# Pairs of heads in a two-layer block's attentions, and ten modulation chunks moved from them into the second projection

## The chip, the cores and the metric

The kernel runs on one core of one Trainium2 chip. The metric is the device time of one execution in microseconds (us). Names of engines: PE is TensorE, DVE VectorE, ACT ScalarE, POOL GpSimd, SP SyncE, which issues most of the transfers.

## The reference, cut to what matters

Two transformer blocks of two layers each work on 256 latent tokens and 256 context tokens of width 1024, in float32. The change touches the first block only. Each of its layers computes, in this order, six modulation vectors, a projection, four mixers side by side (a Fourier mix, "diff" attention, neighbourhood attention "na", a gated MLP along chunks), an output projection and a convolutional feed-forward network. The two attentions are what is changed:

```
m_lat = split(silu(c)     @ w_ada[li] + b_ada[li], 6)      # modulation: 6 x 1024 numbers per stream
m_ctx = split(silu(c_ctx) @ w_ada[li] + b_ada[li], 6)
p, pc = h @ w_in[li], hc @ w_in[li]                          # latent and context tokens
# diff attention, 4 heads: two softmaxes over 32 dimensions each
s = einsum('bhcqd,bhckd->bhcqk', q, k) * 32**-0.5;  a = softmax(s)
o = einsum('bhqk,bhkd->bhqd', a[:, :, 0] - lam * a[:, :, 1], v)      # v has 64 columns per head
# na attention, 4 heads of 64: latent queries see a window (as a bias) and all of the context
a = softmax(concat([q k_local + bias, q k_ctx]) * ...);  o = a v
# context queries (first layer only) see the 256 context keys
```

## The kernel before

**Stream.** All big weights lie in one list of chunks of 1 MB (1024 x 256 floats). SP loads them in order into a ring of four slots (L1155); a slot is free when PE has multiplied with it. A modulation weight is a chunk like any other ("ada" chunk). There are 96 of them for both blocks, and a table of parts (ADA_PARTS) says where in the stream, and so where in PE's program, each is multiplied: 8 at the start, 16 in the first layer's projection, 22 in the first layer's attentions, 17 in the second layer's attentions, the rest in gaps and later. `pe_ada` (L267) does one chunk by eight matmuls of 256 columns whose stationary operands are 32 columns wide, spread over four groups of 32 output partitions of bank 7. The chunks are gathered in batches; when a batch is full ACT copies it to SBUF (L311) and PE turns it by a small matmul (L291) into bank 7's second half.

**Projection.** `pe_in1` multiplies nine chunks of 256 columns with h (L233, L358), and behind some of them does a small piece of the mixers (`pe_slot`: Fourier L383, L392, L393, gMLP L404, square sums L423 and L432). In the first layer two ada chunks follow each of the first eight; in the second none. ACT copies the results out (L732).

**Attentions.** A unit is one head and 128 queries. There are 16 units for the latent queries (eight diff, eight na; 512 keys) and, in the first layer only, 16 more for the context queries (256 keys). All three engines go through the units in a pipeline whose order is written out:

- PE, step u: scores of unit u+1 (L493; for diff two matmuls with 32 rows each, for na one with 64 rows; two sets of two banks in turn), an ada chunk in some steps (L267), transposes of unit u-1 (L505, four or two of 128x128), values of unit u-2 (L520). The values' stationary operand is 128 columns wide and covers two heads; the output is 128 partitions, of which 64 are used.
- DVE: for unit u the add of the window bias (na with latent queries, L595) and the negated maximum (L598); for unit u-1 the reciprocal of the row sums (L609) and the weights (diff L613, L614, L616; na L619); for unit u-3 the copy of the 64 used output partitions to y (L628).
- ACT: for unit u the exponentials with their row sums (L556), for unit u-1 the copy of the transposed weights to WT (L568).

Semaphores tie them: scores of unit u+2 wait for the exponentials of unit u, transposes for the weights, values for the copy to WT and for the copy of the values before. Behind the last unit DVE squares the diff outputs (L838), PE sums them (L670) and goes on to the output projection (L663).

## Time and profile before

| | us |
|---|---|
| median of three runs | 2966.58 (2956.06 to 2972.48) |
| the profiled execution | 2964.01 |
| its span, first to last instruction | 2962.2 |
| mean granted PE clock | 0.979 of full |

| engine | busy us | share |
|---|---|---|
| PE matmul | 2822.7 | 95% |
| PE weight load (beside it) | 2232.1 | 75% |
| DVE | 1575.8 | 53% |
| POOL | 926.6 | 31% |
| ACT | 675.4 | 23% |

The span is from the first to the last instruction of one profiled execution; 1.8 us lie around it. Busy shares are means over stages of different kinds. The chain that ended last is followed back from the last instruction; in each stage it says which engine set the end. A line of it has a start, a length and how many records are merged ("x4"). A float32 matmul leaves two records, a transpose one. The granted clock is the share of full clock that PE was given; 1.00 is 2.4 GHz, 0.50 is 1.2 GHz.

### The profile page before, as it was taken

Reading aid. Unit: us, or ns where it says so; the run is one execution under the profiler, and the core shown is the slowest. Engines: PE = TensorE matmul, PEld = TensorE weight load, DVE = VectorE, ACT = ScalarE, POOL = GpSimd, SP = SyncE. Lnnn points to the kernel's source line nnn. Section 1 sums busy time; section 2 is a strip of 40 time slices with the busy share of each in tenths; the row PEclk is TensorE's granted clock in tenths of the full one; section 3 lists DMA queues with packets and bytes.
Section 4 is the critical chain, followed back from the end, with each engine's and each line's share of the span. In section 5 each row is a group of like instructions: output and inputs, shape, how many; then the busy total and the mean of one; then the engine's idle time right before and its main releaser. Section 6 shows DMA issues by size and latency. Waiting matters only on the chain.

```text
span 2962.2 us, 41023 instructions
## 1 busy us (share of the span) xinstructions
PE 2822.7 (95%) x16033; PEld 2232.1 (75%) x16033; DVE 1575.8 (53%) x2664; ACT 675.4 (23%) x1386; POOL 926.6 (31%) x705
## 2 busy tenths in 40 slices
PE   7999999999899999999978889999999999999999
PEld 3566488888666799744448889788688886698899
DVE  2237378773235588555567775684545122224772
ACT  1124121110123221133235555320100002321000
POOL 1000045554200166300134442553455440020565
PEclk8999999999999999999999999999999999999999
DMA  7447222222415544534432231312122223111443
GB/s 292 170 170 259 111 73 92 92 86 100 156 71 211 188 157 170 207 141 164 124 97 76 73 87 40 118 72 86 71 90 95 86 86 130 60 44 44 152 163 127
DMA packets 108360, 357.82 MB, mean 121 GB/s; under 512 B 41200, under 2 KB 60400, under 8 KB 69136
## 3 DMA queue, kind: packets, MB, share of 16 engines
q1 hardware_dynamic: 86432, 334.65, 32.1%
q10 hardware_dynamic: 20160, 15.40, 1.6%
q0 software_dynamic: 1584, 5.21, 0.6%
q8 instruction: 127, 2.08, 0.3%
q14 instruction: 57, 0.47, 0.1%
HBM read 344.62 MB, written 10.62 MB: 120 GB/s over the span
## 4 chain that ended last, share of the span: by engine, by line
PE 81%; DVE 9%; ACT 4%; DVEq 2%; issue 2%; DMA 2%; POOLq 0%; POOL 0%; ACTq 0%; SPq 0%
PE psum L2955 38%; PE psum L233 16%; PE psum L358 4%; PE psum L267 3%; PE psum L663 3%; PE psum L2506 2%; PE psum L493 1%; ACT h_sb L1116 1%; PE psum L520 1%; DMA ring<-in_stream 1%; PE psum L1640 1%; PE psum L1622 1%; PE psum L2607 1%; PE psum L505 1%; DVE arena L1063 1%
## 5 line engine op out<-in xcount | busy, mean ns | idle before, releaser
L2955 PE MATMUL psum<-arena,ring 128*128 128x256 f32 (+1 forms) x3128 | 559.1, 331 | 0.9 <-DVE arena L3033 0.9
L2955 PEld LDWEIGHTS psum<-arena,ring 128*128 128x128 f32 x3128 | 488.8, 191 | 45.0 <-DVE arena L3033 1.5
L233 PE MATMUL psum<-h_sb,ring 128*128 128x512 f32 (+1 forms) x1248 | 480.3, 543 | 20.7 <-ACT h_sb L1116 18.0
L233 PEld LDWEIGHTS psum<-h_sb,ring 128*128 128x128 f32 x1248 | 238.9, 194 | 250.6 <-issue 228.1
L2955 PE MATMUL psum<-arena,c 128*128 128x256 f32 (+1 forms) x1952 | 359.2, 333 | 1.7 <-DVE c L2974 1.7
L2955 PEld LDWEIGHTS psum<-arena,c 128*128 128x128 f32 x1952 | 308.8, 191 | 31.6 <-issue 1.9
L2983 POOL TENSOR_TENSOR rows<-ring 128x512 f32<-128x512 f32 (+1 forms) x70 | 89.8, 1283 | 621.6 <-DVE arena L3013 333.5
L2983 POOL TENSOR_TENSOR c<-ring 128x512 f32<-128x512 f32 (+1 forms) x73 | 95.1, 1303 | 597.6 <-PE psum L2955 283.9
L2955 PE MATMUL psum<-h_sb,ring 128*128 128x256 f32 (+1 forms) x1264 | 227.5, 334 | 1.0 <-DVE arena L1063 0.8
L2985 POOL TENSOR_TENSOR ring<-ring 128x512 f32<-128x512 f32 x143 | 216.1, 1511 | 23.4 <-issue 3.5
L2999 ACT COPY kst<-psum 128x256 f32<-128x256 f32 (+1 forms) x99 | 31.7, 320 | 837.1 <-PE psum L2955 812.2
L2955 PEld LDWEIGHTS psum<-h_sb,ring 128*128 128x128 f32 x1264 | 199.6, 193 | 20.5 <-issue 1.9
L2987 POOL TENSOR_TENSOR c<-ring 128x512 f32<-128x512 f32 x143 | 205.8, 1439 | 20.3
L2140 DVE SCALAR_TENSOR_TENSOR arena<-psum,vec,arena 128x508 f32<-128x508 f32 (+1 forms) x128 | 95.6, 747 | 106.3 <-ACT arena L1849 98.7
L358 PE MATMUL psum<-ring,h_sb 128*128 128x256 f32 x512 | 118.7, 393 | 9.2 <-ACT h_sb L1116 9.2
L267 PE MATMUL psum<-ring,silu_w 128*32 128x256 f32 x1536 | 106.4, 405 | 18.7 <-DMA ring<-in_stream 11.8
L3045 DVE TENSOR_TENSOR h_sb<-kst,psum 128x256 f32<-128x256 f32 (+1 forms) x20 | 7.3, 365 | 215.0 <-ACT kst L2999 215.0
L358 PEld LDWEIGHTS psum<-ring,h_sb 128*128 128x128 f32 x512 | 98.2, 195 | 31.1 <-ACT h_sb L1116 7.2
L267 PEld LDWEIGHTS psum<-ring,silu_w 128*32 128x32 f32 x1536 | 43.0, 113 | 88.1 <-issue 45.0
L2955 PE MATMUL psum<-arena,rows 128*128 128x256 f32 (+1 forms) x552 | 105.3, 333 | 0.3 <-POOL gates L2990 0.3
L2955 PEld LDWEIGHTS psum<-arena,rows 128*128 128x128 f32 x552 | 88.3, 191 | 8.6 <-POOL gates L2990 0.7
L2091 POOL TENSOR_TENSOR arena<-arena,c 128x512 f32<-128x512 f32 x12 | 17.0, 1440 | 239.7 <-DMA arena<-gsums 239.7
(362 smaller groups left out, 4418.1 us busy)
## 6 DMA issues: line engine op xcount, KB each, us to landing
ring<-in_stream SPq DMA_DIRECT2D x302, 1024.0 KB, 4.8
arena<-decays SPq DMA_DIRECT2D x24, 256.0 KB, 4.9
ring<-gsums SPq DMA_DIRECT2D x20, 256.0 KB, 4.2
keys_d<-kst ACTq DMA_DIRECT2D x16, 256.0 KB, 3.9
arena<-gsums SPq DMA_DIRECT2D x12, 256.0 KB, 4.3
x_sb<-in_x ACTq DMA_DIRECT2D x1, 2048.0 KB, 19.2
arena<-in_rpb POOLq DMA_DIRECT2D x32, 64.0 KB, 8.4
keys_d<-c ACTq DMA_DIRECT2D x8, 256.0 KB, 5.0
```

The lines of the kernel that those rows point to most:

```text
L233: ins = pe.matmul(out_ap, lhs(k), rhs(k), start=first and k == 0, stop=last and k == nk - 1)
L267: ins = pe.matmul(bank(7)[32 * j:32 * (j + 1), 0:256], silu[:, a // (2 * ADA_CHUNKS), k, ADA_ROWS - 2 - 2 * q:2 * ADA_ROWS - 2 - 2 * q], w ...
L358: ins = pe.matmul(bank(rho % 4)[:, tt * 256:(tt + 1) * 256], h[:, k, tok:tok + 128], w[:, slot, k, :], start=k == 0, stop=k == KT - 1)
L493: ins = pe.matmul(bank(2 * (u % 2) + c)[:, 0:TOK - st * SEQ], queries[p:p + width], keys[p:p + width], start=True, stop=True)
L663: ins = pe.matmul(bank(rho % 4)[:, 0:tok], w[:, n % RING, k, rho % 2 * 128:(rho % 2 + 1) * 128], y[:, k, 0:tok], start=first and k == ks[0 ...
L2140: ins = dve.scalar_tensor_tensor(z[:, :, lo:hi], u[:, :, lo + shift:hi + shift], b["v"]("dn_conv", 1, 20 * j + 5 * q + 2 + shift), z[:, :, ...
L2506: ins = pe.matmul(bank(rho % 2)[:, tt * 256:(tt + 1) * 256], h[:, k, tok:tok + 128], w[:, (n0 + c) % RING, k, :], start=k == 0, stop=k == ...
L2955: ins = pe.matmul(dst, self.seven_weights(n, i, k, nk), self.seven_moving(x, sums, i, k, nk, width), start=first and j == 0 and k == 0, st ...
L2983: pool.tensor_tensor(s3, a11, a21, ALU.subtract)
L2985: pool.tensor_tensor(a21, a21, a22, ALU.add)
L2987: ins = pool.tensor_tensor(s2, a21, a11, ALU.subtract)
L2999: act.copy(self.out1[:, 0:width], self.seven_bank(item, 0)[:, 0:width]).then_inc(T["first_copied"], 1)
```

## The change

1. Units of na hold two heads: their scores are two matmuls with 64 rows each, on the upper and lower half of the array's rows, in two banks; one maximum, one reciprocal, two scalings and two runs of transposes serve the pair. Units of diff stay one head, but their order is now: both heads of a pair for the same 128 queries, one behind the other.
2. Values are done for two heads at a time: for each 128 keys two matmuls with stationary operands of 64 columns, to output partitions 0-63 and 64-127 of bank 6. All 128 partitions are used; one copy to y for two heads. `WT` becomes two areas with room for two heads each.
3. The first layer has 24 units instead of 32, the second 12 instead of 16. The ada chunks (22 in the first layer) are spread evenly over them.
4. Of the second layer's 17 ada chunks ten are multiplied in its projection instead (two behind each of the first two chunks, one behind each of the next six), seven stay in the attentions. Two batches are turned ahead of the first of the seven. The last square sum of the projection waits for the copy of the batch (ada_copied 6), since it overwrites bank 7.

```diff
 QKV_ADA = [3] * 4 + [2] * 4
-ADA_PARTS = _spans([("ada_first", MIX_ADA), ("ada_in1", 16), ("ada_next0", 22), ("gap1", 2), ("gap2", 4),
-                    ("ada_next1", 17), ("gap3", 3), ("gap4", 4), ("ada_last", sum(QKV_ADA))])
+ADA_PARTS = _spans([("ada_first", MIX_ADA), ("ada_in0", 16), ("ada_next0", 22), ("gap1", 2), ("gap2", 4),
+                    ("ada_in1", 10), ("ada_next1", 7), ("gap3", 3), ("gap4", 4), ("ada_last", sum(QKV_ADA))])
 GAP_AHEAD = {"gap1": 2, "gap2": 0, "gap3": 1, "gap4": 2}
 ADA_BATCHES = [(0, 8), (8, 24), (24, 36), (36, 48), (48, 52), (52, 62), (62, 72), (72, 84), (84, 96)]
+IN1_ADA = ((2, 2, 2, 2, 2, 2, 2, 2, 0), (2, 2, 1, 1, 1, 1, 1, 1, 0))
 TURNED_AT_END = ("ada_first", "gap1", "gap3", "ada_last")
 ADA_ROWS = 2 * max(_end - _first for _first, _end in ADA_BATCHES)
 SILU_COLS = 2 * ADA_ROWS - 2
...
-        WT = area(19456, 1024, z2=2, k=4)
+        WT = [area(at, 1024, z2=2, k=4) for at in (19456, 26560)]
...
@@ -258,7 +261,9 @@
 
             n, a = ada_at(name, i)
             batch, q, last = ada_batch(a)
-            if a > 0 and q == 0 and a not in [ADA_PARTS[part][1] for part in TURNED_AT_END]:
+            if a == ADA_PARTS["ada_in1"][1]:
+                pe_turn(pe, batch - 2)
+            if a > 0 and q == 0 and a not in [ADA_PARTS[part][1] for part in TURNED_AT_END + ("gap2",)]:
                 pe_turn(pe, batch - 1)
             arrived(pe, n)
             for half in range(2):
...
@@ -362,9 +367,8 @@
                         tok = in1_tokens(li, c)
                         k_products(pe, bank(rho % 4)[:, 0:tok], lambda k: w[:, slot, k, half * 128:(half + 1) * 128],
                                    lambda k: h[:, k, 0:tok])
-                if li == 0 and c < IN1_CHUNKS - 1:
-                    for i in range(2):
-                        pe_ada(pe, "ada_in1", 2 * c + i)
+                for i in range(IN1_ADA[li][c]):
+                    pe_ada(pe, f"ada_in{li}", sum(IN1_ADA[li][:c]) + i)
                 pe_slot(pe, li, c)
 
         def pe_slot(pe, li, c):
@@ -425,7 +429,7 @@
                 ins.then_inc(S["rot_ready"], 1)
                 pe.wait_ge(S["qk_sq"], 3 * li + 3)
                 pe_qk_sum(pe, 6, 6)
-                pe.wait_ge(S["ada_copied"], 2 if li == 0 else 5)
+                pe.wait_ge(S["ada_copied"], 2 if li == 0 else 6)
                 pe_qk_sum(pe, 7, 7).then_inc(S["qk_sum"], 1)
 
         def pe_qk_sum(pe, n, b):
@@ -480,46 +484,50 @@
                     dve_square(dve, rho, streams)
 
         def pe_attention(pe, li, units, u0):
+            t0 = 2 * G0[li]
+
             def scores(u):
-                kind, st, hd, qt = units[u]
-                g = u0 + u
+                kind, st, heads, qt = units[u]
                 if u >= 2:
-                    pe.wait_ge(S["exp_done"], g - 1)
-                keys = P[:, (4 if kind == "diff" else 10) + hd // 2, st * SEQ:TOK]
-                queries = P[:, (2 if kind == "diff" else 8) + hd // 2, st * SEQ + qt * 128:st * SEQ + qt * 128 + 128]
-                width, count = (32, 2) if kind == "diff" else (64, 1)
-                for c in range(count):
-                    p = (hd % 2) * 64 + c * 32
+                    pe.wait_ge(S["exp_done"], u0 + u - 1)
+                keys = P[:, (4 if kind == "diff" else 10) + heads[0] // 2, st * SEQ:TOK]
+                queries = P[:, (2 if kind == "diff" else 8) + heads[0] // 2, st * SEQ + qt * 128:st * SEQ + qt * 128 + 128]
+                width = 32 if kind == "diff" else 64
+                for c in range(2):
+                    p = (heads[0] % 2) * 64 + c * width
                     ins = pe.matmul(bank(2 * (u % 2) + c)[:, 0:TOK - st * SEQ], queries[p:p + width], keys[p:p + width],
                                     start=True, stop=True)
                 ins.then_inc(S["scores_ready"], 1)
 
             def transposes(u):
-                kind, st, hd, qt = units[u]
-                g = u0 + u
-                pe.wait_ge(S["weights_ready"], g + 1)
-                if u >= 2:
-                    pe.wait_ge(S["wt_ready"], g - 1)
+                kind, st, heads, qt = units[u]
                 nk = 4 - 2 * st
-                for k in range(nk):
-                    ins = pe.transpose(bank(4 + u % 2)[:, k * 128:(k + 1) * 128],
-                                       EXPO[:, u % 2, 0, k * 128:(k + 1) * 128], ident[:, :])
-                ins.then_inc(S["wt_psum"], 1)
+                for c, hd in enumerate(heads):
+                    t = head_of(units, u) + c
+                    pe.wait_ge(S["weights_ready"], t0 + t + 1)
+                    if t >= 2:
+                        pe.wait_ge(S["wt_ready"], t0 + t - 1)
+                    for k in range(nk):
+                        ins = pe.transpose(bank(4 + hd % 2)[:, k * 128:(k + 1) * 128],
+                                           EXPO[:, u % 2, c, k * 128:(k + 1) * 128], ident[:, :])
+                    ins.then_inc(S["wt_psum"], 1)
 
             def values(u):
-                kind, st, hd, qt = units[u]
-                g = u0 + u
-                pe.wait_ge(S["wt_ready"], g + 1)
-                if u >= 1:
-                    pe.wait_ge(S["o_copied"], g)
+                kind, st, heads, qt = units[u]
+                if heads[-1] % 2 == 0:
+                    return
+                g = head_of(units, u) // 2
+                pe.wait_ge(S["wt_ready"], t0 + 2 * g + 2)
+                if g >= 1:
+                    pe.wait_ge(S["o_copied"], G0[li] + g)
                 nk = 4 - 2 * st
                 vs = 6 if kind == "diff" else 12
-                p = (hd % 2) * 64
                 for k in range(nk):
                     kt = 2 * st + k
-                    ins = pe.matmul(bank(6)[:, 0:128],
-                                    P[:, vs + kt // 2, (kt % 2) * 256 + (hd // 2) * 128:(kt % 2) * 256 + (hd // 2) * 128 + 128],
-                                    WT[:, u % 2, k, :], start=k == 0, stop=k == nk - 1)
+                    for j in range(2):
+                        v0 = (kt % 2) * 256 + (heads[-1] // 2) * 128 + 64 * j
+                        ins = pe.matmul(bank(6)[64 * j:64 * j + 64, 0:128], P[:, vs + kt // 2, v0:v0 + 64],
+                                        WT[g % 2][:, j, k, :], start=k == 0, stop=k == nk - 1)
                 ins.then_inc(S["o_ready"], 1)
...
@@ -584,29 +598,26 @@
             neg_lam = small[:, 4:5]
 
             def maxima(u):
-                kind, st, hd, qt = units[u]
-                g = u0 + u
-                dve.wait_ge(S["scores_ready"], g + 1)
+                kind, st, heads, qt = units[u]
+                dve.wait_ge(S["scores_ready"], u0 + u + 1)
                 b = 2 * (u % 2)
                 n = TOK - st * SEQ
-                count = 2 if kind == "diff" else 1
+                scores = bank(b, 2).rearrange("p (c k) -> p c k", c=2)[:, :, 0:n]
                 if kind == "na" and st == 0:
-                    part = bank(b)[:, 0:SEQ]
-                    dve.tensor_tensor(part, part, NAB[:, hd, qt, :], ALU.add)
+                    part = scores[:, :, 0:SEQ]
+                    dve.tensor_tensor(part, part, NAB[:, heads[0]:heads[0] + 2, qt, :], ALU.add)
                     dve.drain()
-                scores = bank(b, count).rearrange("p (c k) -> p c k", c=count)[:, :, 0:n]
-                dve.tensor_reduce(small[:, 8 + b:8 + b + count], scores, AX.X, ALU.max, negate=True)\
+                dve.tensor_reduce(small[:, 8 + b:10 + b], scores, AX.X, ALU.max, negate=True)\
                    .then_inc(S["max_ready"], 1)
 
             def weights(u):
-                kind, st, hd, qt = units[u]
-                g = u0 + u
-                dve.wait_ge(S["exp_done"], g + 1)
+                kind, st, heads, qt = units[u]
+                dve.wait_ge(S["exp_done"], u0 + u + 1)
                 n = TOK - st * SEQ
                 b = 12 + 2 * (u % 2)
                 r = small[:, 16:18]
                 dve.drain()
-                dve.reciprocal(r[:, 0:2 if kind == "diff" else 1], small[:, b:b + (2 if kind == "diff" else 1)])
+                dve.reciprocal(r, small[:, b:b + 2])
                 dve.drain()
                 e = EXPO[:, u % 2]
                 if kind == "diff":
@@ -616,17 +627,18 @@
                     dve.scalar_tensor_tensor(e[:, 0, 0:n], e[:, 1, 0:n], small[:, 18:19], e[:, 0, 0:n],
                                              ALU.mult, ALU.add).then_inc(S["weights_ready"], 1)
                 else:
-                    dve.tensor_scalar(e[:, 0, 0:n], e[:, 0, 0:n], r[:, 0:1], None, ALU.mult)\
-                       .then_inc(S["weights_ready"], 1)
+                    for c in range(2):
+                        dve.tensor_scalar(e[:, c, 0:n], e[:, c, 0:n], r[:, c:c + 1], None, ALU.mult)\
+                           .then_inc(S["weights_ready"], 1)
 
             def copy_o(u):
-                kind, st, hd, qt = units[u]
-                g = u0 + u
-                dve.wait_ge(S["o_ready"], g + 1)
-                p = (hd % 2) * 64
+                kind, st, heads, qt = units[u]
+                if heads[-1] % 2 == 0:
+                    return
+                dve.wait_ge(S["o_ready"], G0[li] + head_of(units, u) // 2 + 1)
                 tok = st * SEQ + qt * 128
-                dve.tensor_copy(y[p:p + 64, (2 if kind == "diff" else 4) + hd // 2, tok:tok + 128],
-                                bank(6)[p:p + 64, 0:128]).then_inc(S["o_copied"], 1)
+                dve.tensor_copy(y[:, (2 if kind == "diff" else 4) + heads[-1] // 2, tok:tok + 128],
+                                bank(6)[:, 0:128]).then_inc(S["o_copied"], 1)
 
             n = len(units)
             for u in range(n + 3):
@@ -641,11 +653,15 @@
         def units_of(li):
             out = []
             for st in range(2 if li < DEPTH - 1 else 1):
-                out += [(kind, st, hd, qt) for kind in ("diff", "na") for hd in range(4) for qt in range(2)]
+                for half in range(2):
+                    for qt in range(2):
+                        out += [("diff", st, (2 * half + j,), qt) for j in range(2)]
+                out += [("na", st, (2 * half, 2 * half + 1), qt) for half in range(2) for qt in range(2)]
             return out
 
         UNITS = [units_of(li) for li in range(DEPTH)]
         U0 = [0, len(UNITS[0])]
+        G0 = [0, head_of(UNITS[0], len(UNITS[0])) // 2]
 
         def pe_mixers1(pe, li):
...
@@ -3447,10 +3463,9 @@
         w_in = _chunks(i["w_in"][li])[list(IN1_ORDER)]
         if li == 0:
             stream.append(ada[:MIX_ADA])
-            for c in range(IN1_CHUNKS - 1):
-                stream.append(np.stack([w_in[c], *ada[MIX_ADA + 2 * c:MIX_ADA + 2 * c + 2]]))
-            w_in = w_in[IN1_CHUNKS - 1:]
-        stream.append(w_in)
+        for c in range(IN1_CHUNKS):
+            first = ADA_PARTS[f"ada_in{li}"][0] + sum(IN1_ADA[li][:c])
+            stream.append(np.stack([w_in[c], *ada[first:first + IN1_ADA[li][c]]]))
         stream.append(ada[slice(*ADA_PARTS[f"ada_next{li}"])])
         stream.append(_chunks(i["w_out"][li]))
         stream.append(ada[slice(*ADA_PARTS[f"gap{2 * li + 1}"])])
```

## Rows read from the trace of the kernel before

**Rows 1.** Windows: length, busy PE, PEld, DVE, ACT, POOL; clock, DMA share, GB/s.

```profile
914.00:976.00 62.00, 59.24 (x521) 35.04 (x522) 40.98 (x90) 26.21 (x66) 0.00 (x0) 1.00 0.84 305
```

**Rows 2.** The chain: start, us, engine, line, records. Second layer's attentions, 512 keys.

```profile
931.45 1.06 PE psum L493 x4
932.50 1.00 PE psum L267 x16
933.50 0.59 PE psum L505 x4
934.09 0.89 PE psum L520 x8
...
950.17 0.55 PE psum L291 x4
...
956.74 1.05 PE psum L493 x2
```

**Rows 3.** The chain, first layer's attentions of context queries, 256 keys.

```profile
284.96 0.37 PE psum L505 x2
285.33 0.45 PE psum L520 x4
285.78 0.63 PE psum L493 x2
```

**Rows 4.** The chain at the start and end of both attention stretches.

```profile
205.70 1.15 PE psum L493 x4
...
209.64 2.08 PE psum L493 x4
...
212.71 1.87 PE psum L267 x16
...
300.38 3.27 PE psum L670 x4
...
914.18 1.15 PE psum L493 x4
...
975.61 1.98 PE psum L670 x4
```

**Rows 5.** Windows, columns as in rows 1, behind the first scores of both layers.

```profile
212.00:214.00 2.00, 2.00 (x20) 1.17 (x19) 1.76 (x5) 0.00 (x0) 0.00 (x0) 0.50 0.00 0
...
916.00:918.00 2.00, 1.71 (x22) 0.94 (x20) 1.71 (x2) 1.39 (x5) 0.00 (x0) 1.00 0.91 385
```

**Rows 6.** The chain in the first (to 114 us) and second layer's projection.

```profile
72.81 1.86 PE psum L267 x32
...
113.21 0.63 PE psum L392 x2
...
836.76 0.43 PE psum L392 x2
...
853.95 2.50 PE psum L404 x32
...
882.43 13.81 PE psum L358 x64
```

**Rows 7.** VectorE in order of time (start, us, line, operation): three reciprocals.

```profile
921.01 0.17 DVE L609 RECIPROCAL small<-small 128x2 f32<-128x2 f32 x1
...
923.86 0.17 DVE L609 RECIPROCAL small<-small 128x2 f32<-128x2 f32 x1
...
926.90 0.17 DVE L609 RECIPROCAL small<-small 128x2 f32<-128x2 f32 x1
```

**Rows 8.** Groups by line and shape on VectorE, 918 to 975: busy us, mean ns.

```profile
L598 DVE TENSOR_REDUCE small<-psum 128x2 f32<-128x1024 f32 x6 | 7.3, 1219 | 0.8 <-PE psum L493 0.8
...
L598 DVE TENSOR_REDUCE small<-psum 128x1 f32<-128x512 f32 x8 | 5.5, 691 | 0.6
...
L595 DVE TENSOR_TENSOR psum<-psum,arena 128x256 f32<-128x256 f32 x8 | 3.5, 433 | 5.4 <-PE psum L493 5.4
```

**Rows 9.** Rate in 40 slices of 20 to 80 us, early ada chunks and projection.

```profile
GB/s 388 421 399 415 437 421 426 421 399 421 431 429 406 435 408 389 216 194 194 27 0 0 0 0 0 76 377 426 426 426 366 11 0 0 0 27 208 426 421 426
```

More of the change, by code:

```diff
@@ L165, in build_program @@
         DATA1 = CONST1 + C1["end"]
-        assert DATA1 + D1["end"] <= 28672
+        assert DATA1 + D1["end"] <= 26560
         def c1(name, n=128):
@@ L248, in ada_at @@
             first, end = ADA_PARTS[name]
-            if name == "ada_in1":
-                return in1_chunk(0, i // 2) + 1 + i % 2, first + i
+            if name in ("ada_in0", "ada_in1"):
+                li = int(name[-1])
+                c = [i < sum(IN1_ADA[li][:j + 1]) for j in range(IN1_CHUNKS)].index(True)
+                return in1_chunk(li, c) + 1 + i - sum(IN1_ADA[li][:c]), first + i
             if name == "ada_last":
@@ L539, in pe_attention, with head_of @@
                     pe_ada(pe, ada, i)
+        def head_of(units, u):
+            return sum(len(units[i][2]) for i in range(u))
         def next_ada_at(li, u, units):
@@ L561, in copy_wt @@
             def copy_wt(u):
[L562 to L569 removed]
+                kind, st, heads, qt = units[u]
+                nk = 4 - 2 * st
+                for c, hd in enumerate(heads):
+                    t = head_of(units, u) + c
+                    g = t // 2
+                    act.wait_ge(S["wt_psum"], t0 + t + 1)
+                    if g >= 2:
+                        act.wait_ge(S["o_ready"], G0[li] + g - 1)
+                    act.copy(WT[g % 2][:, hd % 2, 0:nk, :], bank(4 + hd % 2)[:, 0:nk * 128].rearrange("p (k q) -> p k q", k=nk))\
+                       .then_inc(S["wt_ready"], 1)
             n = len(units)
```

27 lines of the change are left out of this document (10 added, 17 removed).

## The prediction

> **What bounds the kernel now.** I read the busy shares first, then the chain that ended last over each of the two attention stretches and the projections beside them, then the same seconds on VectorE, then granted clock and DMA by windows. TensorE (PE) is busy over 95% of the span, and in the second layer's attentions 59.2 of 62 us [rows 1]. The chain there is one PE step after the other. A step of a unit with 512 keys is scores 1.06, a modulation chunk 1.00, transposes 0.59, values 0.89 [rows 2]. With 256 keys it is 0.63, 1.00, 0.37, 0.45 [rows 3]. Turning a batch is 0.55. So what PE drops from a step is gained until VectorE or a wait is next. The first layer's attentions run from 205.70 to the sums of squares at 300.38, the second's from 914.18 to 975.61 [rows 4].
>
> **Scores by pairs.** A diff unit has two matmuls on two row groups of 32 (four records) in 1.06; an na unit has one with 64 rows (two records) in 1.05 [rows 2]. The two halves of diff thus run at once, and I price a pair of na heads, on rows 0-63 and 64-127 and in two banks, like diff: 1.06 for two heads (0.63 with 256 keys). Eight na pairs with 512 keys save 8 x 1.05 = 8.4, four with 256 keys 4 x 0.63 = 2.5. By layer: first 4.2 + 2.5, second 4.2.
>
> **Values by pairs.** Today each head multiplies both heads' columns and half is thrown away: two heads cost 1.78 (0.90). New: eight matmuls with 64 columns each, alternating between two column halves of one bank. No row shows just that, so bounds. Below: perfect overlap, half of 1.78, is 0.89. Above: no overlap, 1.78 + 0.2 for the change of tile shape = 1.98. Between lie two rows. The modulation chunk alternates four column groups: 16 records of 256 columns in 1.00. At the plain rate, 13.81 for 64 such records [rows 6], they would need 3.45 one after the other, 0.86 four at once: full overlap and 0.14 for the new shape. The gMLP, with 64 columns but four matmuls in a row on one half, needs 2.50 for 16, or 1.25 for eight [rows 6]. Change of shape back costs the next operation 0.2: the same two matmuls take 0.63 behind a chunk and 0.43 without it [rows 6]. The order here alternates as the chunk's does, so I take 0.85 + 0.18 = 1.03 for 512 keys and 0.43 + 0.17 = 0.60 for 256. A saving of 0.75 and 0.30 for each two heads: first layer 8 x 0.75 + 8 x 0.30 = 8.4, second 6.0.
> The Trainium skill speaks against it here: "TensorEngine Tiling (Array Packing)", Key Properties, says that changing the tiling mode drains the engine; the trace agrees, with the 0.2 above. "TensorE: Matmul & The Clock Gate", Measured speedup, has 2.38 times for three column tiles instead of 3; an estimate by that share would be 1.78 / 1.59 = 1.12 for the pair, and 2 us less gain in all.
>
> **First layer.** PE drops 6.7 + 8.4 = 15.1. Its 22 chunks now fall on 24 steps instead of 32. Can the others follow? VectorE's pace is seen where it runs free: reciprocal to reciprocal 2.85, and 3.04 with a copy of an output [rows 7]; the copy is now in every second unit, so 2.95. PE's mean diff step is 1.06 + 1.00 + 0.59 + 0.52 = 3.17: PE still leads. In na pairs VectorE has the add (0.43 for 256, I take 0.70 for 512), one reduction 1.22 for both (two of 0.69 today) [rows 8], small steps and two scalings, together 3.55 by the same spacing; PE has 1.06 + 1.00 + 1.18 + 1.03 = 4.27. With 256 keys PE's diff step is 0.63 + 1.00 + 0.37 + 0.30 = 2.30, and VectorE's 2.95 less at least 0.53 for the shorter reduction, at most 2.4: even. So the first layer gains PE's 15.1. ScalarE has two exponentials and two copies in an na pair, under 3 us, no bound.
>
> **Second layer's attentions.** PE's sum falls by 4.2 + 6.0 + 10 x 1.00 = 20.2. Not all is gained, as VectorE becomes even with PE. Time from the first scores: the third unit's scores start after 3.93 as today; scores, now two turns (1.10), a chunk and transposes end at 7.7; the next scores, reduction and so the third reciprocal are at 10.1; five further reciprocals at 2.95, and 0.7 for the first na add, 25.5; weights and transposes of the last diff unit 27.8. Four na steps of 3.7, 4.2, 3.3 and 2.2 follow (the later of VectorE's 3.55 and PE's 3.27 or, with a chunk, 4.27; the last has neither scores nor chunk), then today's tail of 4.4. Together 45.6 against 61.4: 15.8 less.
> **The clock.** In the first layer PE has nothing from the end of the second scores (two of 1.0 from 205.70) to the third at 209.64, 1.9 us [rows 4]; chunk and turn come behind them. Its granted clock is then 0.50, the 1.2 GHz level [rows 5], and scores take 2.08, the chunk 1.87 [rows 4]. The second layer today has a turn and a chunk in that gap, and its clock stays at 1.00 [rows 5]. With 7 chunks over 12 units its first step has none: the gap becomes the first layer's. From 209.64 to 212.71 + 1.87 and the transposes behind it took 6.0 where full clock has 3.2; with the second turn, that costs 3.1, and VectorE waits for it. I take it: 15.8 - 3.1 = 12.7.
>
> **The projection.** PE takes over ten chunks, and it is the chain there without a gap: nothing hides them. From the first layer: two chunks in a row 1.86, 0.2 behind them [rows 6]. Two places with two, six with one: 2 x 1.86 + 6 x 1.00 + 7 x 0.2 (the gMLP pays none) = 11.1. Their ten loads leave a stretch with 305 GB/s [rows 1]; they queue on SP only behind loads of the same ring, four deep, and a projection chunk with 512 tokens holds PE for 13.8 [rows 6]: time for five loads. The new wait for batch 6's rows before the last square sums has behind it one matmul; ScalarE copies them while PE does the rotation: nothing. If that cover were gone it would be under 1 us.
>
> **Sum.** 15.1 + 12.7 - 11.1 = 16.7. The profiled execution is 2964.0 (span 2962.2, 1.8 around it): 2947.3. It lies 2.6 under the median of the runs; I give **2947**.
>
> **Rivals.** (1) The two column halves do not overlap as taken. At the gMLP's rate a pair costs 1.40 and 0.77: 16 x 0.37 + 8 x 0.17 = 7 us less gain, 2954. Without overlap 19 us less, 2966, no change. For: one 64-column row, below full overlap. Against: the chunk's row. 0.14.
> (2) No fall of the clock in the second layer: 2944. For: a gap of the same length leaves the second layer's clock alone today, if with work behind it; against: the first layer's row shows the very sequence. 0.12.
> (3) **Slower**: the clock stays low through the second layer's attentions. With PE and VectorE even, shorter steps leave PE short idle stretches, and nothing but such steps follows the first gap. PE's 38 us there would be 75, 30 more than the 46 counted: 2964 + 12 = 2976. It decides from where lost stretches like the first layer's (2.8 us each) number six beyond the one counted. Against: today's narrow steps with 256 keys keep the clock. 0.05.
> (4) Transfers: the first layer's last eleven chunks come every 2.4 us. The chip delivers up to 437 GB/s [rows 9], a chunk in 2.4 us: just even, with four in the ring. At today's 305 GB/s it is 3.4 us, 11 x 1.0 less the ring's lead of some 3: 8 us, 2955. 0.08.
> (5) The change doing nothing of what it says, heads paired but run one after the other on row groups: 11 us less, 2958. 0.02.
> Forecast: 0.57; 0.02 for what I don't see.
>
> **Numbers.** About 0.5%, 15 us, is what a measurement of this kernel can tell from none; the threshold is 2951.7, only 5 under my value, and the three runs shown spread over 16. Forecast band 2939 to 2955, three quarters of it faster. 0.57 x 0.75 + 0.12 x 0.9 + shares of (1) and (4) 0.07 + (5) 0.01 = 0.62 faster, 0.34 same, 0.04 slower. Range: down to 2937 (no fall of the clock, full overlap at 0.89, a fast run), up to 2961 (gMLP rate or transfers, a slow run).
>
> **What would show it.** In the changed profile's chain: scores of an na pair 1.06 with four records; values of a pair at 1.03 (1.4 for rival 1); the first layer's attentions some 79 us from first scores to sums of squares, the second's some 48.7 (45.6 without the clock's fall); the second projection 11 us longer; clock 0.5 behind the second layer's second scores, 1.00 after some 6 us; waits of PE for a landing in the first layer for rival 4. I am wrong if values aren't near 1.03, if VectorE's waits grow in the first layer too, or if the clock falls elsewhere.

## The result and the profile after

The changed kernel takes 2945.15 us (median of 8 runs, 2941.53 to 2951.49) beside 2967.23 of the kernel before on the same chips (8 runs, 2956.06 to 2972.72): a ratio of 0.9931, 95% interval 0.9912 to 0.9950. It is faster, by 22 us in the medians; the profiled executions differ by 18.8 (spans 2962.2 and 2943.4). 2947 had been forecast, with a range of 2937 to 2961.

Where the span's 18.8 us went, by the chains of both kernels (an attention stretch is from its first scores to the first matmul of the squares' sum; the projection from its first matmul to the start of the last copy of its results):

| stretch | before | after | difference | forecast |
|---|---|---|---|---|
| first layer's attentions | 94.68 | 77.16 | -17.5 | -15.1 |
| second layer's projection | 122.33 | 133.45 | +11.1 | +11.1 |
| second layer's attentions | 61.43 | 50.36 | -11.1 | -12.7 |
| the rest of the span | | | -1.3 | 0 |

The rest is 0.5 us less ahead of the first attentions, 1.7 more between them and the second projection, and 2.5 less behind the second attentions.

The chain of the changed kernel in the first layer's attentions is still one PE step behind another. Its lines (start, us, engine, line, records) of a step in the na part, first with 512 keys, then with 256:

```profile
240.72 1.06 PE psum L498 x4
241.78 1.00 PE psum L272 x16
242.78 1.02 PE psum L511 x8
243.80 1.02 PE psum L529 x16
...
270.54 0.63 PE psum L498 x4
271.17 1.00 PE psum L272 x16
272.17 0.59 PE psum L511 x4
272.76 0.59 PE psum L529 x8
```

L498 are the scores, now four records for a pair in 1.06 and 0.63, the same time as the two records of one head in [rows 2] and [rows 3]. L529 are the values of a pair: 16 records in 1.02, eight in 0.59, for which two heads took 1.78 and 0.90 before (twice 0.89, [rows 2], and twice 0.45, [rows 3]). L511 are the transposes of both heads. They take 1.02 and 0.59, not twice 0.59 and twice 0.37. The 0.16 and 0.15 saved are near the 0.2 that a change of tile shape costs in [rows 6], and the pair's transposes start behind such a change once instead of twice; no run takes this part by itself.

Starts and ends of both stretches:

```profile
205.19 1.15 PE psum L498 x8
...
209.12 2.08 PE psum L498 x4
...
282.35 3.11 PE psum L686 x4
```

```profile
908.99 1.15 PE psum L498 x8
...
959.35 1.98 PE psum L686 x4
```

They answer to [rows 4]. The projection of the second layer, with the lines for [rows 6]:

```profile
774.90 11.06 PE psum L363 x50
...
794.93 1.86 PE psum L272 x32
...
825.77 1.00 PE psum L272 x16
826.78 0.63 PE psum L396 x2
827.40 0.43 PE psum L397 x2
```

L272 are modulation chunks, two in a row 1.86, one 1.00; L396 behind one is 0.63 where it is 0.43 without. Nothing hides them: the stretch is 11.1 us longer.

The granted clock in the second layer's attentions (windows: length, busy time and records of PE, weight load, VectorE, ScalarE, GpSimd, then clock, DMA share, GB/s):

```profile
908.99:915.00 6.01, 3.22 (x19) 1.63 (x20) 4.24 (x7) 2.79 (x8) 0.00 (x0) 0.96 0.54 177
915.00:928.00 13.00, 13.00 (x70) 6.21 (x70) 7.59 (x15) 5.55 (x14) 0.00 (x0) 0.50 0.32 108
928.00:959.35 31.35, 27.10 (x275) 15.72 (x273) 24.16 (x49) 17.33 (x43) 0.00 (x0) 1.00 0.52 190
```

For 13 us PE has the 1.2 GHz level, and its steps in the chain show it; from 929 on the chain runs through VectorE:

```profile
918.31 2.01 PE psum L498 x4
920.32 1.05 PE psum L511 x4
921.37 2.01 PE psum L498 x4
923.37 1.86 PE psum L272 x16
...
929.31 1.22 DVE small L610
...
938.83 1.23 DVE small L610
```

Scores take 2.01, a chunk 1.86, transposes 1.05. The lines of VectorE behind them (L610 reductions; VectorE's own sequence) have no counterpart in the chain of before in this layer. They had one in its first layer: in the diff units of the context queries the chain of before ran through VectorE from 269.38 to 275.87. In the changed kernel that stretch is gone.

### The profile page after: what moved, and what is told of

The parts are those of the page before. It is cut to its first block, busy times and chain, and to the rows that moved or that the text cites. A ratio compares the mean times of both kernels' runs of the same rounds, so it can differ in the third digit from the quotient of the medians.

```text
span 2943.4 us, 40895 instructions
## 1 busy us (share of the span) xinstructions
PE 2797.6 (95%) x16033; PEld 2207.0 (75%) x16033; DVE 1559.4 (53%) x2608; ACT 674.2 (23%) x1386; POOL 925.9 (31%) x705
## 3 DMA queue, kind: packets, MB, share of 16 engines
q8 instruction: 127, 2.08, 0.3%
## 4 chain that ended last, share of the span: by engine, by line
PE 80%; DVE 9%; ACT 5%; DVEq 2%; issue 2%; DMA 1%; POOLq 0%; ACTq 0%; POOL 0%; SPq 0%
PE psum L2971 38%; PE psum L234 16%; PE psum L363 4%; PE psum L272 3%; PE psum L679 3%; PE psum L2522 2%; ACT h_sb L1132 1%; DMA ring<-in_stream 1%; PE psum L1656 1%; PE psum L498 1%; PE psum L1638 1%; PE psum L2623 1%; PE psum L511 1%; PE psum L529 1%; DVE arena L1079 1%
## 5 line engine op out<-in xcount | busy, mean ns | idle before, releaser
L272 PE MATMUL psum<-ring,silu_w 128*32 128x256 f32 x1536 | 109.3, 415 | 18.4 <-DMA ring<-in_stream 11.8
L272 PEld LDWEIGHTS psum<-ring,silu_w 128*32 128x32 f32 x1536 | 44.0, 116 | 88.1 <-issue 46.0
```

What stands on the lines that cost most here:

```text
L272: ins = pe.matmul(bank(7)[32 * j:32 * (j + 1), 0:256], silu[:, a // (2 * ADA_CHUNKS), k, ADA_ROWS - 2 - 2 * q:2 * ADA_ROWS - 2 - 2 * q], w ...
```

## Experiments

Two explanations had to be told apart. **Mine**: the pairs make the whole gain; moving ten chunks costs more than it brings, since a chunk is 1.1 us in the projection and at most 1.0 in the attentions; and the second layer lost what VectorE and a clock at half kept back. **The rival**: the move takes load off attentions that otherwise would be bound by the ring's transfers or by VectorE, and is a part of the gain. Medians and stretches of all kernels (us; "clock low" is a granted clock of 0.50 somewhere in the stretch, in the one profiled execution of each; a fall of the clock is its change from 1.00 to 0.50). A ratio is to the kernel before as measured together with it. That kernel's median was 2967 to 2968 each time but with filler_full, filler_full2 and combined_full, where it was 2963.1; there the ratios are the fairer comparison.

| kernel | median | ratio to before | attentions 1 | attentions 2 | clock low in 1, in 2 |
|---|---|---|---|---|---|
| before | 2967.2 | 1 | 94.7 | 61.4 | yes, no |
| changed | 2945.2 | 0.9931 (0.9912 to 0.9950) | 77.2 | 50.4 | yes, yes |
| pairs_only | 2937.6 | 0.9905 (0.9886 to 0.9923) | 79.3 | 50.4 | yes, no |
| move_only | 2973.2 | 1.0022 (1.0012 to 1.0031) | 94.7 | 58.7 | yes, yes |
| first_chunk | 2936.9 | 0.9899 (0.9883 to 0.9915) | 77.1 | 43.6 | yes, no |
| runs | 2951.4 | 0.9945 (0.9928 to 0.9962) | 81.2 | 53.6 | yes, yes |
| values_wide | 2961.8 | 0.9972 (0.9959 to 0.9985) | 91.6 | 57.1 | yes, yes |
| combined | 2930.3 | 0.9860 (0.9840 to 0.9881) | 78.3 | 49.8 | yes, no |
| both_first | 2935.3 | 0.9877 (0.9856 to 0.9899) | 73.5 | 43.6 | no, no |
| filler | 2945.7 | 0.9917 (0.9898 to 0.9937) | 77.7 | 51.8 | yes, yes |
| filler_full | 2943.8, one run | | 74.5 | 50.4 | no, yes |
| filler_full2 | 2940.4 | 0.9914 (0.9897 to 0.9930) | 74.5 | 46.2 | no, briefly |
| combined_full | 2931.5 | 0.9888 (0.9870 to 0.9906) | 74.6 | 50.7 | no, no |

### One part alone: pairs without the move

```diff
-("ada_in1", 10), ("ada_next1", 7)
+("ada_in1", 0), ("ada_next1", 17)
-IN1_ADA = ((2, ..., 0), (2, 2, 1, 1, 1, 1, 1, 1, 0))
+IN1_ADA = ((2, ..., 0), (0,) * IN1_CHUNKS)
...
```

The places of the turns and the wait for the batch's copy (ada_copied) are again those of the kernel before.

> The changed kernel with the pairs of heads, but all 17 modulation chunks of the second layer left in its attentions, as before the change. My theory: the pairs make all of the gain and the move costs more than it gives. A chunk costs PE 1.00 us in the attentions and 1.1 in the projection, and in the attentions some of it fills time in which PE would wait for VectorE. The second projection is 11.1 us shorter than in the changed kernel (122.3 instead of 133.4), the second layer's attentions take about 50 us, no longer than the 50.4 of the changed kernel, since PE leads again and its clock does not fall (the first step has a turn and a chunk in it). In all some 2934 us. Rival one, the move pays: without it the attentions take the 60 us that ten chunks more make of 50.4, and the time is that of the changed kernel, 2945, or more. Rival two, transfers: 17 chunks in 50 us is one in 2.9 us, in the diff part one in 2.6, about what the ring delivers at best; then PE waits for landings over 5 us in all, and the time is 2939 or more.

Measured 2937.6, 7.5 us under the changed kernel, and five of its six runs lie under the lowest of the changed kernel's eight; 2934 was expected. The second layer's attentions take 50.4 us with 17 chunks as with 7. The missing 3.5 us lie where both kernels have the same code: in the profiled execution 1.2 us ahead of the first layer's attentions and 2.2 in them (79.3 instead of 77.2), where the clock was low until 14.5 us after the first scores and in the changed kernel until 9.6. Behind the second layer's attentions the clock fell once more, but from there to the end only 0.2 us are lost. The windows of the attentions and of what follows:

```profile
901.00:951.50 50.50, 46.95 (x520) 25.09 (x520) 36.19 (x70) 25.79 (x66) 0.00 (x0) 1.00 0.96 372
951.50:960.00 8.50, 8.49 (x28) 6.03 (x29) 1.31 (x2) 2.17 (x2) 0.00 (x0) 0.81 0.05 18
```

372 GB/s at a DMA share of 0.96 is a high rate beside the 437 of [rows 9], yet no wait of PE for a landing is among the waits of that stretch. PE is busy for 46.95 of 50.5 us. So both rivals fall: the move does not pay, and the transfers sufficed. That ten chunks more cost nothing in this stretch is in part the clock's doing, since the changed kernel loses time to its fall there. With the clock at 1.00 in both (combined and both_first below) they cost 6.3 us, 49.8 against 43.6, which is still less than 11.1 in the projection.

### The other part alone: the move without pairs

The kernel before with the edits to ADA_PARTS, IN1_ADA, in1_chunk, ada_at, pe_ada, pe_in1, ScalarE's copy of the batches, the wait for it and the stream of the diff, and nothing of the attentions.

> The kernel before with the move of ten chunks alone, heads one by one. My theory: it is slower. The second projection grows by 11.1 us; the attentions shrink by 10 us of PE less some 3 in which VectorE (3.04 a diff unit, PE 2.54 without a chunk) now leads and less some 3 by the clock, which falls in the first step without a chunk: 57 us instead of 61.4. In all about 2974, ratio 1.002. Rival: the move alone gives part of the measured gain: under 2963.

Measured 2973.2, ratio 1.0022 (1.0012 to 1.0031): slower by 5 to 6 us, as expected. The second layer's attentions went from 61.4 to 58.7 only (57 was expected) while the projection had ten chunks more. The clock there was 0.91 in the mean, and in the chain VectorE led for much of the stretch:

```profile
929.04 2.08 PE psum L497 x4
...
936.00 1.87 PE psum L272 x16
...
944.15 1.13 DVE small L602
```

Scores (L497) with 2.08 and a chunk (L272) with 1.87 are at the lower level; L602 is VectorE's reduction. The part of the change that was meant to relieve the attentions is a loss by itself: 2.8 us gained in them, 11.1 spent in the projection.

### A chunk in the second layer's first step

The seven chunks come one step earlier where the spread allows; with the first of them both turns move into the first step. The edit, shortened:

```diff
-return list(range(min(u, units) * count // units, min(u + 1, units) * count // units))
+if li == 1:   # rounded up instead of down: steps 0, 1, 3, ... have the seven chunks
+    return list(range(-(-min(u, units) * count // units), -(-min(u + 1, units) * count // units)))
```

> The changed kernel with the second layer's seven chunks one step earlier each where the spread allows, so that the first step has the two turns and a chunk between second and third scores. Nothing else differs. My theory: the clock stays at full through the second layer's attentions and they take 45.6 us instead of 50.4, in all some 2940.5. Rival one: the clock falls anyway, for the steps are thin, and nothing changes (2945). Rival two: the clock stays, but VectorE sets the end in any case, and under 1.5 us are gained.

Measured 2936.9, 8.3 us under the changed kernel and more than the 4.7 expected: both the fall's price and my estimate without it were off. The window of the attentions, and their chain at start and end:

```profile
907.20:950.80 43.60, 37.34 (x361) 20.84 (x361) 35.65 (x70) 25.57 (x64) 0.00 (x0) 1.00 0.55 194
```

```profile
907.20 1.15 PE psum L498 x8
...
950.79 1.98 PE psum L689 x4
```

43.6 us at a clock of 1.00, with the same instructions as in the changed kernel's 50.4. Not all of the 6.8 us between them is the fall. The last reciprocal of the changed kernel and of first_chunk:

```profile
952.07 0.17 DVE L620 RECIPROCAL small<-small 128x2 f32<-128x2 f32 x1 [0.34 <-ACT arena L568]
```

```profile
944.23 0.17 DVE L623 RECIPROCAL small<-small 128x2 f32<-128x2 f32 x1 [0.34 <-ACT arena L571]
```

From there to the squares' sum the changed kernel takes 7.28 us and first_chunk 6.56, both at full clock: with the chunks one step earlier none is left for the last step. These 0.7 us are the chunk's place, and the fall cost at most 6.1. VectorE's reciprocals are the pace of this stretch; four of the na part:

```profile
932.29 0.17 DVE L623 RECIPROCAL small<-small 128x2 f32<-128x2 f32 x1
936.12 0.17 DVE L623 RECIPROCAL small<-small 128x2 f32<-128x2 f32 x1
939.24 0.17 DVE L623 RECIPROCAL small<-small 128x2 f32<-128x2 f32 x1
942.56 0.17 DVE L623 RECIPROCAL small<-small 128x2 f32<-128x2 f32 x1
```

3.83 behind the last diff unit, then 3.12 and 3.32 for an na pair, where I had 3.55.

### The order of the values' matmuls

```diff
-for k in range(nk):
-    for j in range(2):      # column halves alternate
+for j in range(2):          # all of one half, then all of the other
+    for k in range(nk):
```

> The changed kernel with the values' eight (four) matmuls in another order: all those of the first head, then all of the second, instead of alternating; the same matmuls on the same column halves. My theory: what lets the two halves run at once is the alternation. In runs of four a pair costs what the gMLP's rate gives, 1.40 us instead of 1.02 (0.77 instead of 0.59 with 256 keys): 8 x 0.38 + 8 x 0.18 = 4.5 us more in the first layer and about 2 in the second, where VectorE leads: some 2951. Rival: the order does not matter, 1.02 and 2945. Other rival: no overlap at all in runs, 1.9 us a pair, 2958.

Measured 2951.4: 6.3 us over the changed kernel, 6 had been expected. By the stretches it was 4.0 us in the first layer and 3.3 in the second, where 4.5 and 2 had been expected. The chain has the price of the order:

```profile
220.65 1.51 PE psum L529 x16
```

```profile
277.00 0.59 PE psum L529 x8
```

With four matmuls of a head in a row the pair takes 1.51 instead of 1.02; with two in a row 0.59, no more than when they alternate. So alternation matters where a run is four long; my 1.40 from the gMLP was 0.11 too low, and my 0.77 for 256 keys wrong. 8 x 0.49 = 3.9 us, nearly all of the 4.0 by which the first layer's attentions grew; that the total was met is two errors against each other.

### Values as before

The values go head by head again, with 128 columns each (shortened):

```diff
-for k in range(nk):
-    for j in range(2):
+for j in range(2):
+    for k in range(nk):
...
-ins = pe.matmul(bank(6)[64 * j:64 * j + 64, 0:128], P[:, ..., v0:v0 + 64], WT[g % 2][:, j, k, :], ...)
+ins = pe.matmul(bank(6)[:, 128 * j:128 * j + 128], P[:, ..., v0:v0 + 128], WT[g % 2][:, j, k, :], ...)
-dve.tensor_copy(y[:, kt, tok:tok + 128], bank(6)[:, 0:128])
+for j in range(2):
+    dve.tensor_copy(y[64 * j:64 * j + 64, kt, tok:tok + 128], bank(6)[64 * j:64 * j + 64, 128 * j:128 * j + 128])
```

> The changed kernel, but values as before the change: for each head a stationary operand of 128 columns, of whose outputs half is used (now in two stretches of the bank, copied by two instructions for a pair). Only the part with the two column halves is undone. My theory: a pair costs 1.78 instead of 1.02 (0.90 instead of 0.59), the change of shape ahead of it is saved (within these numbers): 8 x 0.76 + 8 x 0.31 = 8.5 us more in the first layer, which PE leads, and some 3 in the second, where VectorE leads: 2945 + 11 = 2956. Rival: the values don't matter, since waits take their place: under 2950.

Measured 2961.8, 16.7 us more than the changed kernel: more than expected, but the steps are as priced:

```profile
220.04 2.01 PE psum L498 x4
...
232.10 1.79 PE psum L529 x16
...
269.58 0.89 PE psum L529 x8
```

A pair's values 1.79 and 0.89; 8 x 0.77 + 8 x 0.30 = 8.6 us of the first layer's 14.4. Another part is the clock: its scores are at 2.01 still at 220.04, where the changed kernel is back at full clock by 215. From 215.12 to 224.96 its chain has two rounds of scores, chunk and transposes in 9.84 us, for which the changed kernel takes 5.29 (215.02 to 220.31). That is 4.6 us; the last 1.2 lie, by difference, in the tail behind the last unit, with values of 1.14 and two copies for a pair. Why the clock stayed low longer here, no run shows. The column halves bring at least these 8.6 us in the first layer, more than the 6.7 at which the scores by pairs were priced there (those weren't undone alone).

### What holds the clock

Three kernels tried to name what lets the clock fall. In **filler** the second unit's scores are multiplied twice in the first step of both layers; in **filler_full** and **filler_full2** one and two matmuls over all rows are done there (`pe.matmul(bank(6), ones, h[:, 0, :])`, output never read).

> The changed kernel with the chunks where they are, but in the first step of each layer's attentions the second unit's scores are multiplied twice into the same banks, so that PE has 1 us more to do in the gap ahead of the third scores. It is work for nothing; no chunk is earlier. My theory: what costs is the clock that falls after the gap, not where the chunk is. With half of the gap filled the clock stays at full in the second layer, and its attentions take some 44 us instead of 50.4 although PE does more; the first layer's take 74.4 to 75 instead of 77.2; in all some 2936. Rival: filling it with thin matmuls doesn't hold the clock, and the time is 2945, or it holds it and the gain of first_chunk came from the chunk's place: attentions of the second layer at 48 us or more with the clock at 1.00.

> The changed kernel with one matmul over all 128 rows and 512 columns for nothing in the first step of each layer's attentions (0.87 us at full clock; its output is never read). The traces so far: the first two units' scores, on four row groups, are done in 1.15 us in the changed kernel where they took 2.0 before, so PE's gap ahead of the third scores is 2.8 us and not 1.9; the repeated scores (filler) only made it 1.9 again, and the clock fell. This one leaves 1.9 too. If the length of the gap decides, the clock falls in the second layer again and its attentions take 50 to 52 us. If it is the kind of work (thin scores against full rows), the clock holds, and they take some 44.

> As filler_full with two such matmuls (1.74 us), so that the gap is about 1.05 us. Chunks stay where the changed kernel has them. If the length of the gap decides, the clock now holds in the second layer: attentions 43.6 us as in first_chunk though no chunk is earlier, and in the first layer 73.5 to 77; in all 2935 to 2939. If the place of the chunk made first_chunk's gain, the second layer's attentions stay at 48 or more with the clock at 1.00. If the clock falls even so, 50 and 2945.

A surprise lies ahead of them all. The kernel before (first layer), the changed kernel (first and second layer) and filler (second layer), matmuls in order of time, with the idle time ahead of them in brackets:

```profile
205.70 1.99 PE L493 MATMUL psum<-arena 32*128 32x512 f32 x8 [0.68 <-ACT arena L732]
```

```profile
205.19 1.14 PE L498 MATMUL psum<-arena 32*128 32x512 f32 x8 [0.68 <-ACT arena L748]
209.12 2.08 PE L498 MATMUL psum<-arena 32*128 32x512 f32 x4 [2.79 <-ACT arena L568]
...
908.99 1.14 PE L498 MATMUL psum<-arena 32*128 32x512 f32 x8 [0.68 <-ACT arena L748]
912.92 1.13 PE L498 MATMUL psum<-arena 32*128 32x512 f32 x4 [2.79 <-ACT arena L568]
```

```profile
906.40 2.00 PE L498 MATMUL psum<-arena 32*128 32x512 f32 x12 [0.68 <-ACT arena L751]
910.34 2.07 PE L498 MATMUL psum<-arena 32*128 32x512 f32 x4 [1.94 <-ACT arena L571]
```

The new order of the diff units puts both heads of a pair behind each other. They lie on four different row groups, so the first two units' scores, eight records, take 1.14 us where they took 2.0 before. The work ends earlier, the exponentials do not, and PE's gap in the first layer grew from 1.95 to 2.79; in the second it was 0.41 before, with turn and chunk in it, and is 2.79 too. The repeated scores made it 1.94 again, as in the first layer before, and the clock fell as it did there (2945.7: expectation missed). The two others, filler_full in the upper fence and filler_full2 in the lower, each with the first layer ahead of the second (windows with the clock in the third last column):

```profile
205.00:216.00 11.00, 8.59 (x65) 3.70 (x66) 8.00 (x15) 5.60 (x15) 0.00 (x0) 1.00 0.47 163
...
900.00:930.00 30.00, 27.57 (x148) 15.04 (x146) 14.52 (x27) 11.18 (x30) 0.00 (x0) 0.77 0.29 105
```

```profile
205.00:216.00 11.00, 9.45 (x67) 3.93 (x65) 7.68 (x13) 5.30 (x14) 0.00 (x0) 1.00 0.40 145
...
900.00:930.00 30.00, 27.63 (x188) 15.64 (x190) 17.65 (x34) 13.60 (x35) 0.00 (x0) 0.94 0.36 131
```

filler_full (one run) left 1.74 us of gap in both layers. In the first the clock held (attentions 74.5), in the second it fell (50.4). With 0.88 us left (filler_full2) it held in the first and was low for a short time in the second (46.2 instead of 50.4). So the gap's length alone does not decide, nor the kind of work alone; shorter gaps fell less often and for less long. The chunk's place in first_chunk was not the cause of its gain by itself: filler_full2 has the chunks where the changed kernel has them and still won 4.1 us in that stretch, with 3.4 us of low clock left in it. What does decide whether the clock falls stays open.

### Both ideas together

combined is pairs_only with the chunks rounded up in both layers, both_first the changed kernel with the same rounding, combined_full is combined with one full matmul for nothing in each first step.

> Pairs of heads without the move (as pairs_only), and in both layers the modulation chunks are spread so that the first step has one. In the second layer nothing changes by that (17 chunks over 12 units have one there already but for the rounding). In the first layer the turn and a chunk fill the gap between second and third scores, in which the clock falls in every run so far. My theory: the clock stays at full there, and its attentions take 77.2 - 2.8 = 74.4 us or a little less; the second layer's take 50.4 as in pairs_only. In all some 2934, 3 to 4 us under pairs_only. Rival: the chunk's load has not landed or the clock falls anyway: 2937.6 as pairs_only.

> The changed kernel, ten chunks moved, with a chunk in the first step of both layers. Against combined it differs only in the move. My theory: first layer as in combined (74.4), second as in first_chunk (attentions 43.6, projection 133.4): 43.6 + 11.1 - 50.4 = 4.3 us longer than combined, 2.8 shorter than first_chunk: some 2934 by first_chunk's 2936.9, so combined should come out at 2930 to 2934. Rival: the move costs nothing net, and both are equal.

> combined (pairs of heads, no chunk moved, a chunk in the first step of both layers) with one full-row matmul for nothing in each first step. In combined's trace 1.2 us of gap were left in the first layer behind turn and chunk, and the clock fell (attentions 78.3); in both_first the same code had the same gap and it did not fall (73.5). With the matmul 0.4 us are left. Theory: the clock holds, the first layer's attentions take 73.5, the second's 50: a span of 2927.8 - 4.8 = 2923, median some 2926 to 2928 by combined's 2930.3. Rival: in most of combined's executions the clock already holds, and the median moves by less than 1.5 us.

combined takes 2930.3 and both_first 2935.3, where 2934 had been expected of each: without the move it is 5.0 us faster, 4.3 had been expected. The four runs of one overlap with the four of the other, so this pair says little by itself. The stretches say the same more firmly: the projection is 11.1 us shorter without the move and the second layer's attentions, both at full clock, 6.3 longer, 4.8 net.

combined is 14.9 us faster than the changed kernel, but not for the reason that I had: the first layer's clock should have held, and in the profiled execution it fell. Its span is 8.0 us shorter than that of pairs_only, of which 1.6 lie in the two attentions; the rest lies where the code is the same. Behind the second layer's attentions all these kernels have one code, and it took 1981.6 us in combined, 1984.1 in the changed kernel, 1984.3 in pairs_only and 1988.9 in both_first. What chunks in the first steps are worth to the whole is therefore not shown by these medians. In combined and both_first the first step of the first layer is the same, with the same gap of 1.23 us, and yet:

```profile
205.00:216.00 11.00, 9.62 (x60) 3.56 (x64) 6.66 (x12) 4.82 (x14) 0.00 (x0) 0.70 0.69 242
```

```profile
205.00:216.00 11.00, 9.23 (x84) 3.98 (x88) 8.29 (x15) 6.33 (x17) 0.00 (x0) 1.00 0.83 286
```

The upper is combined, the lower both_first: a clock of 0.70 in one and 1.00 in the other, 78.3 and 73.5 us for the same work. combined_full, with 0.37 us of gap, had 1.00 and 74.6, but its median is 2931.5, no better than combined. My expectation of 2926 to 2928 was missed. In the second layer its weight loads waited 2.6 us in all for landings of the ring (combined 1.9, pairs_only none), though its matmuls themselves waited only 0.6, and the chain runs through two transfers from 897.51 to 913.59: with 17 chunks the transfers are near to being the next limit. And low clock turned up elsewhere: right behind the first layer's attentions (280 to 284) the clock is 0.57 in the mean in combined_full, where combined's is 1.00 behind its own. Against combined its profiled execution won 3.8 us in the first layer's attentions and lost 0.9 in the second's, 1.0 between them and 4.5 behind them (1986.1 against 1981.6), in the same code. Whether filling the gap causes these losses, or they are chance, is open.

## Why the prediction was right, point by point

- **Scores by pairs**: 1.06 and 0.63 for two heads, as taken.
- **Values by pairs**: 1.03 and 0.60 taken, 1.02 and 0.59 measured. The nearest row, the modulation chunk's four alternating column groups, was the right one; the gMLP's was the price of another order, as runs showed. Rival 1 is out. The estimate of 1.12 from the Trainium skill ("TensorE: Matmul & The Clock Gate", Measured speedup) was too high; the trace gives 1.02, so the row was the better guide here. The drain at a change of tiling mode that the Trainium skill states ("TensorEngine Tiling (Array Packing)", Key Properties) agrees with L396's 0.63 behind a chunk, 0.43 without.
- **First layer**: 15.1 forecast, 17.5 measured. Missed was that a pair's transposes are cheaper than those of two heads: 1.18 was taken, 1.02 measured, 4 x 0.16 + 4 x 0.15 = 1.2 us. The tail is another 0.5 shorter, from the last transposes to the squares' sum 3.4 us instead of 3.9. And the working took PE to lead throughout before the change; the chain of before runs through VectorE from 269.38 to 275.87, with a wait of 0.24 and a step longer by 0.3, and this 0.5 is gone. After the change VectorE didn't lead, as forecast.
- **Projection**: 11.1 and 11.1. The sum of 1.86, 1.00 and 0.2 from the other layer's rows held to a tenth.
- **Second layer's attentions**: 12.7 forecast, 11.1 measured, but from two errors against each other. Without a fall I had 45.6; first_chunk has 43.6, and 44.3 with the 0.7 of its earlier chunks put back. Its third reciprocal comes at 9.7 us where I had 10.1, and an na pair costs VectorE 3.1 to 3.3 and not 3.55. The fall of the clock was foreseen from the missing chunk in the first step, but its price was a mis-sized term: 3.1 us forecast, up to 6.1 measured (44.3 against 50.4). The gap had grown to 2.79, which I had not seen. The clock fell later than forecast, behind the third scores (still 1.13) and not ahead of them, and stayed low until 928, 13 us where I had some 6.
- **Rival 3**, the clock low through the whole stretch, did not come: it was low for 13 of 50 us. **Rival 4**, transfers: no stall in the changed kernel (0.3 us of a weight load in the first layer); it begins to show only where 17 chunks fall on twelve units at full clock.
- **The sum**: 16.7 forecast, 18.8 between the spans, 22.1 between the medians. That the sum is so near is partly luck: the first layer gained 2.4 us more than forecast, the second layer's attentions 1.6 less. The rest of 1.3 us is in no stage of the change; executions differ by more than that in stages with the same code.
- **What the sum hid**: I costed the move at 11.1 against 10 us of PE and did not ask what it would be without it. The same terms say it: VectorE's pace and the clock gave back most of the ten. pairs_only shows that the second layer's attentions are as long with 17 chunks, and at full clock the ten are worth 6.3 us there.

## What to carry to other kernels

Narrow matmuls on different row groups or column halves can run at once. On two column halves they did so best when they alternated, no worse with two in a row on one side, less well with four in a row. Price them by a row of the trace with the same order, not merely of the same shape, and look for operations whose change of shape is now paid once. Work moved from a stretch to another is worth only what the first stretch's other engines let go: move it out only if that engine still leads afterwards, and time each part of a change alone. Work that fills the gap at the start of a pipeline may be worth more than its own time, by the clock it keeps up, but whether the clock holds has to be read in several executions.

## What the runs showed of the hardware that was not expected

- Scores of two diff heads on four row groups of 32: eight records of 512 columns in 1.14 us, as long as four of them.
- Four matmuls in a row on one column half, then four on the other: 1.51 us, alternating 1.02, all with 128 columns: 1.79. Two in a row: 0.59, alternating 0.59, with 128 columns 0.89.
- A gap of 1.2 us let the clock fall in one execution (combined) and not in another (both_first) at the same place of the same code; a gap of 1.74 held in one layer and not in the other (filler_full). What a fall costs differs as much: the second layer's attentions took 43.6 us without it (0.7 of the difference is the chunks' place), 46.2 with 3.4 us at the lower level, 50.4 with 13 us.
- While the clock was low for these 13 us (915 to 928 in the changed kernel) PE was busy all the time, with thin scores, transposes and chunks.
- The same code behind the second layer's attentions took 1981.6 us in one profiled execution (combined) and 1988.9 in another (both_first); their mean granted clocks over the whole span are 0.984 and 0.980.
